# Prompt attention: each round's scores ahead of its transposes on TensorE

## What is computed

```python
s = jnp.einsum('...qkgd,...skd->...kgqs', qg, k)
s = s * (hd ** -0.5) + rel_bias(dist, rel_table)
s = jnp.where(mask, s, -jnp.inf)          # 0 <= dist <= 128, valid keys
m = jnp.maximum(jnp.max(s, axis=-1, keepdims=True), sink)
p = jnp.exp(s - m)
den = jnp.sum(p, axis=-1, keepdims=True) + jnp.exp(sink - m)
o = jnp.einsum('...kgqs,...skd->...qkgd', (p / den).astype(v.dtype), v)
```

## Time and profile before

| | us |
|---|---|
| median of 3 runs (2396.84 to 2398.55) | 2398.39 |
| the profiled execution, its own time | 2398.73 |
| its span, first to last instruction | 2396.6 |
| TensorE busy in it | 2374.7 (99%) |
| VectorE busy | 1004.5 (42%) |
| ScalarE busy | 570.8 (24%) |
| GpSimd busy | 112.1 (5%) |

### The profile page before, as it was taken

The page is one execution under the profiler, slowest core; times in us unless marked ns, Lnnn a source line. Parts: engine busy times, 40 slices in busy tenths (PEclk is TensorE's granted clock), DMA queues, the critical chain, the costliest instruction groups (busy, mean ns, idle before and its releaser), DMA issues.

```text
span 2396.6 us, 35127 instructions
## 1 busy us (share of the span) xinstructions
PE 2374.7 (99%) x15129; PEld 2311.1 (96%) x15129; DVE 1004.5 (42%) x1408; ACT 570.8 (24%) x1016; POOL 112.1 (5%) x131
## 2 busy tenths in 40 slices
PE   8999999999999999999999999999999999999998
PEld 8997899999999999999999998889999999999998
DVE  6449724433433333335623325545343343343333
ACT  6549722111111111103310116422111111110111
POOL 1005400000000000000000004100000000000000
PEclk9999999999999999999999999999999999999999
DMA  8621031111111111111321136431111111111112
GB/s 226 86 48 72 11 100 53 36 53 36 53 35 53 42 46 52 36 45 43 102 65 36 36 108 178 135 124 36 53 53 36 53 35 53 46 41 51 36 36 73
DMA packets 133016, 150.30 MB, mean 63 GB/s; under 512 B 33421, under 2 KB 107177, under 8 KB 132764
## 3 DMA queue, kind: packets, MB, share of 16 engines
q1 hardware_dynamic: 129980, 136.11, 19.2%
q0 software_dynamic: 2720, 12.56, 1.7%
q10 hardware_dynamic: 224, 0.30, 0.0%
HBM read 126.50 MB, written 24.47 MB: 63 GB/s over the span
## 4 chain that ended last, share of the span: by engine, by line
PE 96%; DVE 1%; ACT 1%; issue 0%; DMA 0%; DVEq 0%; SPq 0%
PE ps L316 42%; PE ps L323 21%; PE ps L300 8%; PE ps L304 7%; PE ps L301 7%; PE ps L551 1%; PE ps L1033 1%; PE ps L1009 1%; PE ps L990 1%; ACT prob L1101 1%; PE ps L2080 1%; PE ps L1410 1%; PE ps L1411 1%; PE ps L1412 1%; PE ps L2061 1%; PE ps L2065 1%
## 5 line engine op out<-in xcount | busy, mean ns | idle before, releaser
L1537 DVE TENSOR_TENSOR x<-x,ps 128x1074 f32<-128x1074 f32 (+1 forms) x128 | 161.8, 1264 | 453.5 <-PE ps L323 453.5
L264 ACT ACTIVATE w_hi<-raw 128x1024 fp32r<-128x1024 f32 x180 | 187.4, 1050 | 648.6 <-PE ps L323 485.6
L316 PE MATMUL ps<-act_hi,w_hi 128*128 128x352 f32 (+2 forms) x1536 | 334.4, 326 | 0.0
L316 PE MATMUL ps<-act_hi,w_lo 128*128 128x352 f32 (+2 forms) x1536 | 333.7, 325 | 0.0
L316 PE MATMUL ps<-h_hi,w_lo 128*128 128x352 f32 (+2 forms) x1536 | 333.5, 325 | 0.0
L316 PE MATMUL ps<-h_hi,w_hi 128*128 128x352 f32 (+2 forms) x1536 | 333.4, 325 | 0.0
L323 PE MATMUL ps<-act_lo,w_hi 128*128 128x352 f32 (+2 forms) x1536 | 273.7, 324 | 0.0
L1519 DVE SCALAR_TENSOR_TENSOR relu<-ps,rstd 128x1074 f32<-128x1074 f32 (+1 forms) x64 | 81.1, 1266 | 447.4 <-PE ps L323 447.4
L316 PEld LDWEIGHTS ps<-act_hi,w_lo 128*128 128x128 f32 x1536 | 265.0, 189 | 0.0
L316 PEld LDWEIGHTS ps<-h_hi,w_lo 128*128 128x128 f32 x1536 | 263.8, 189 | 0.0
L316 PEld LDWEIGHTS ps<-h_hi,w_hi 128*128 128x128 f32 x1536 | 263.6, 189 | 0.0
(11 more groups left out here) (324 smaller groups left out, 2363.0 us busy)
## 6 DMA issues: line engine op xcount, KB each, us to landing
raw<-in_mlp_w_up SPq DMA_DIRECT2D x32, 1024.0 KB, 5.5
raw<-in_mlp_w_down SPq DMA_DIRECT2D x32, 1024.0 KB, 5.0
raw<-in_mlstm_w_in SPq DMA_DIRECT2D x12, 1024.0 KB, 5.4
x<-scratch_x SPq DMA_DIRECT2D x8, 537.0 KB, 6.0
scratch_x<-x POOLq DMA_DIRECT2D x1, 4296.0 KB, 14.0
x<-scratch_x SPq DMA_DIRECT2D x8, 528.0 KB, 4.7
x_tok<-in_x_prompt SPq DMA_DIRECT2D x8, 512.0 KB, 7.8
raw<-in_attn_w_qkv SPq DMA_DIRECT2D x16, 256.0 KB, 6.7
```

Of the source, the lines that this page charges most:

```text
L264: nc.scalar.activation(unit_view(w_hi, slot, down), raw_unit(j, rslot, down), ACT.Copy).then_inc(w_hi_ready, 1)
L316: nc.tensor.matmul(ps[:, bank + g, 0:c.stop - c.start], w_block(w, slot, k, kc, cols), hi[:, k, c], start=start and i == 0, stop=False)
L1537: nc.vector.tensor_tensor(view(x[:, o, :]), view(x[:, o, :]), ps[:, out_banks(n):out_banks(n) + 3, 0:w], ALU.add).then_inc(out_free, 1)
```

## The change

In `att_pe`, the transposes of item n-4 are issued behind the scores of item n, except in round 6 where they stay at the head. As the cached keys' transposes and the sample's scores stand ahead of the prompt's scores in the code, the transposes of items 32 to 35 come behind these in rounds 36 to 38.

```diff
         def att_pe(pe):
             for n in range(2, NG + LAG + 1):
-                if LAG + 2 <= n < NG + LAG:
+                if n == LAG + 2:
                     att_transpose_pe(pe, n - LAG)
                 if NG <= n < NG + 2:
                     turn_k_pe(pe, 2 * (n - NG))
...
                 if n < NG:
                     att_scores_pe(pe, n)
+                if LAG + 3 <= n < NG + LAG:
+                    att_transpose_pe(pe, n - LAG)
                 if n == 3:
```

## The result

The median went from 2398.64 us (20 runs) to 2401.7 us (20 runs): a ratio of 1.0014 with an interval of 1.0008 to 1.002. That is 3.1 us or 0.13%, inside the 0.2% that was called no change, and inside the range; the value forecast was 2400.7. The profiled execution took 2402.25 us, its span is 2400.1. Behind the edit the lines are two higher (L1009, L990 and L1033 stay; L1085 is now L1087, L1129 now L1131, L1149 now L1151, L1260 now L1262, L1266 now L1268, L1301 now L1303, L1410 now L1412).

What follows compares the result with a forecast made beforehand. TensorE bounds the kernel, busy 2374.7 of 2396.6 us. First rounds -0.65, middle +1.2 and -0.5 make about 0; the tail adds 2.35: +2.3 us, 2400.7, range 2397.3 to 2403.5.

Steps and rivals of the forecast that it cites:

- The bound and the sign: Attention stage: under 4 us of TensorE stalls to win; whole change forecast slower by 2.3 us.
- A steady round: Full rounds: S, T, V still takes 3.11 us; ScalarE and VectorE run 1.06 us later.
- Rival 3: Every round longer, 3.11 to say 3.25 us, through semaphore latency: 3.9 us atop 2.3, 2404.6; chance 0.05.
- First rounds: Round 7: S(7) fills T(3)'s 1.49 us wait; V(2) starts about 188.5 instead of 189.15, gain 0.65 us.
- Middle: V(14)'s wait behind VectorE's spreading grows, +0.65 to +1.2, taken 1.2; T(20), T(24) give -0.5; sum to round 35 about 0.
- S can fill both: T(20)'s 0.18 and T(24)'s 0.51 us waits for ScalarE are filled by scores: -0.5 to -0.7, taken -0.5.
- no wait: Steady rounds: S never waits for the minimum pass two rounds back, done at t+3.9 against 6.2.
- Tail: Rounds 36 to 39: stalls of 1.65 us ahead of cache transposes and 0.6 ahead of sample's scores; V(35) +2.35 us.
- The lower bound: End of the stage: cost of the new order if ScalarE and VectorE were not late, +1.2 us.
- Rival 1: Tail hidden from the shift, gaps of T(3), T(20), T(24) filled: -0.6 us, 2398.1; chance 0.30 together with no change.
- Rival 2: Rounds 37 and 38: stall plus transposes drop the clock to half, losing 3.4 us atop 2.3: 2404.1; chance 0.08.

Runs made afterwards that it cites:

- experiment 8: The best version: kernel before with T(3), T(20), T(24) behind their scores and only the spreading's clearing moved to round 9; 2395.87 us against 2398.51, ratio 0.9994.
- experiment 1: Kernel before with only T(32) to T(35) behind the sample's work, T(3) to T(31) still ahead of the scores; 2400.13 us, ratio 1.0011.
- experiment 2: Kernel before with only T(3) to T(31) behind the scores, T(32) to T(35) still ahead of the sample's work; 2399.72 us, ratio 1.0009.
- experiment 3: Changed kernel with T(33) alone moved back ahead of the cache transposes of round 37; 2400.7 us, ratio 1.0012 against the kernel before.
- the second of 7: Kernel before with VectorE's spreading moved from round 18 to rounds 9, 10, 11 and T(3), T(20), T(24) behind their scores; ratio 1.0.
- third kernel of experiment 7: Kernel before with VectorE's spreading moved from round 18 to rounds 9, 10, 11 and T(3) to T(31) behind their scores; ratio 1.0008.
- experiment 6: Kernel before with only T(3), T(20) and T(24) behind their scores; 2397.8 us against 2397.49, ratio 0.9997.

## Why the prediction was right, and where it was off

**The bound and the sign** held. The stage had under 4 us to win, and it lost 3.19 (forecast 2.3), less than the 4.8 us that counted as a change. The size is right in part by luck: in the middle a gain of 0.7 us and waits of 0.8 us, neither of which the forecast had, nearly cancel.

**A steady round, 3.11 us and a shift of 1.06 us**: held to the digit. The denominator was put at about t+5.27 or just behind, and stands at t+5.30; the copy and the minimum pass are each 1.06 us later. VectorE's waits for the last exponential rose from 3.0 us in 5 times to 5.8 in 14, the mark of an engine that now follows another. Rival 3 (every round longer) falls with it: from V(14) to V(18) each V stands the same 0.08 us ahead of before.

**First rounds**: -0.65 forecast; what stands ahead of V(2) began 4.93 us from T(2) instead of 5.71, -0.78, and V(2) itself 5.24 instead of 6.08, -0.84. S(7) waited for item 5's minimum pass, as said. What the forecast put at nothing: rounds 7 to 13 also hold transposes for the values and caches (L853, L858), and they cost less behind T than behind S. Round 8, before and then after:
```profile
190.54 1.09 PE L1009 MATMUL ps<-cst,prob 128*128 128x128 f32 x8
...
192.63 0.44 PE L853 MATMUL ps<-cst,vT 128*128 128x128 f32 x2
193.00 1.09 PE L1033 MATMUL ps<-probT,v_tok 128*64 128x128 f32 x16
```
```profile
190.07 1.14 PE L990 MATMUL ps<-kn,q 64*128 64x256 f32 x8
...
192.06 0.38 PE L853 MATMUL ps<-cst,vT 128*128 128x128 f32 x2
192.37 1.09 PE L1033 MATMUL ps<-probT,v_tok 128*64 128x128 f32 x16
```
From the round's start to V it is 2.46 us before and 2.30 after. Rounds 8 to 12 gain 0.12 to 0.15 us each, so V(9) stands 1.56 us earlier than before.

**Middle**: the sum said 0, it was +0.47 (V(31) at 94.60 instead of 94.13 us from T(2)), in these steps. S(15) waited 0.34 us, which the forecast had not: V(10) is 1.14 us early instead of V(9)'s 1.56. At V(14) the lead went from 1.11 us (V(13)) to 0.08, a loss of 1.03; its wait grew by 1.06 (0.73 to 1.79), as the shift says. So this term, 0.65 to 1.2, taken as 1.2, was sized about right, and the stall ate more lead than the forecast knew of. Then the step "S can fill both" gaps, of T(20) and T(24), failed: both scores waited themselves, 0.29 and 0.50 us, for the minimum pass of two items back, and V(23) stood 0.11 us later than before: +0.19 where -0.5 was taken. S(33) waited 0.29, the rest of the 0.47.

I had freed S of that wait ("no wait", done at t+3.9 against 6.2) with the row of a full round and the pass where it stood before the shift. In the new phase the pass ends near t+5.0, so 1.2 us of room are left, and around the meta blocks two rounds together are shorter by more than that. Rounds 22 and 23, after:
```profile
234.63 1.13 PE L990 MATMUL ps<-kn,q 64*128 64x256 f32 x8
235.69 0.26 PE L1009 MATMUL ps<-cst,prob 16*16 16x16 f32 x4
```
T(18) takes 0.19 us from start to start instead of 1.02, and in round 23 V(18) takes 0.33 instead of 1.03. Without its wait S(24) would start some 4.7 us behind S(22) (it started at 239.64, 5.01 behind), and the pass is not done by then. Rounds 31 and 32 are alike ahead of S(33). In rounds 13 and 14, ahead of S(15), the copies of the transposes for the caches delay VectorE as well. Ahead of round 28 it is another thing: VectorE's small sum of item 25 takes 1.29 us instead of 0.16, and ends with GpSimd's scaling, as in experiment 8; it took 1.29 before the change too.
```profile
247.62 1.89 POOL L1121 TENSOR_TENSOR prob<-prob,stat 128x1024 f32<-128x1024 f32 x1
248.25 1.29 DVE L1093 TENSOR_TENSOR stat<-sinks,stat 128x4 f32<-128x4 f32 x1
```

**Tail**: +2.35 forecast, 2.71 us measured: from V(31) to V(35) it was 277.57 to 288.54, 10.97 us, and is 278.40 to 292.08, 13.68 us. The two waits are right in place and size, 1.60 for 1.65 and 0.62 for 0.6; the wait of T(35) for the copy of T(34), 0.18 (0.25 with the overlap lost), and 0.1 inside the sample's scores were missed. The lower bound, +1.2 for a tail without the shift, was too low as well: experiment 1, which is that tail, gives +1.65. Sum of the parts: 0.47 + 2.71 = 3.18.

**The rivals.** Rival 1 fell at both ends: the gaps only changed hands, and the shift reached the tail. Rival 2, the clock: in round 37, 1.60 us of waiting and 1.9 us of transposes stood in a row, and the windows after say 1.00 there:
```profile
275.00:285.00 10.00, 7.78 (x92) 6.65 (x91) 7.81 (x29) 8.12 (x25) 5.68 (x3) 1.00 0.19 57
310.00:311.00 1.00, 1.00 (x8) 1.00 (x8) 0.00 (x0) 0.00 (x0) 0.00 (x0) 0.59 0.00 0
316.00:317.00 1.00, 1.00 (x5) 1.00 (x5) 0.00 (x0) 0.00 (x0) 0.00 (x0) 0.50 1.01 412
317.00:318.00 1.00, 1.00 (x8) 1.00 (x7) 0.00 (x0) 0.00 (x0) 0.00 (x0) 0.99 1.02 417
```
The clock stayed at 2.4 GHz; the first fall is the one of before: it begins at 310.2, during the sample's values, and ends at 317.0. The Trainium skill's "TensorE: Matmul & The Clock Gate" ("Part 4: PE-mode transpose") says that transposes do not count as activity the way matmuls do. No fall followed here, so this stretch of fp32 transposes doesn't bear it out, or it was too short to show it.

**What stays open**: the account of the scores' waits behind the meta blocks (two short rounds) is read from the trace, not tested by an edit, and so is GpSimd's part in the slow small sum and the slow copies. Why a pair of transposes costs less behind T than behind S is not shown.

## What to carry to other kernels

Here three engines ran within 0.2 us of the same period, and swapping two groups on one of them didn't change the period, only the phase of the engines that follow. In such a case read who is a microsecond later, and follow that to every place where the pattern breaks (short items, an inserted job, the end). A group of work that stands ahead of a wait is its cover: when it is moved behind, the wait shows at full length and the group's own followers are late as well. In this kernel only the groups that wait were worth moving: three moved groups of transposes took 0.74 us off the stage, all 33 of them added 3.19. And work that is taken out of an engine's list frees its time only if what stands behind it can start earlier and run as fast: 0.9 us of clearing gave 0.25.

## What the runs showed that I had not expected

The kernel's time comes in steps. The half-rate stretch of TensorE that begins during the sample's values lasted 6.8 us before (306.3 to 313.2) and after, but 3.4 us in the profile of experiment 1:
```profile
308.00:309.00 1.00, 1.00 (x9) 1.00 (x9) 0.00 (x0) 0.00 (x0) 0.00 (x0) 0.77 0.00 0
309.00:311.00 2.00, 2.00 (x9) 2.00 (x9) 0.99 (x4) 1.68 (x5) 0.00 (x0) 0.50 0.39 54
311.00:312.00 1.00, 1.00 (x5) 1.00 (x5) 0.72 (x1) 0.25 (x1) 0.00 (x0) 0.52 0.90 322
```
3.4 us less at half rate are 1.7 us of time, and that profile's span is 2396.4 us although its stage is 1.65 us longer than before (2396.6). Over all twelve profiles the stretch is 3.4 us in five (experiments 1, 2, 3, the second of 7, and 8), 6.8 in six, and 10.2 in the third kernel of experiment 7, whose mean clock is 0.997. The 20 runs of the changed kernel fall into the same steps: 2399.9 to 2400.4 (8 runs, mean clock 0.999), 2401.6 to 2402.3 (8 runs, 0.998), 2402.9 to 2403.6 (4 runs, 0.997), with nothing between. So two single spans can differ by the whole effect of such a change, and the interval of a ratio over mixed steps is as wide as the effect. Compared at the same mean clock, 0.999, with the kernel before in the same comparison, the times follow the stage: the best version's median is 2395.74 against 2396.85, -1.1 us for -1.04 of its stage; experiment 6's is 2396.08 against 2397.06, -1.0 for -0.74; experiment 1's is 2398.63 against 2397.06, +1.6 for +1.65. These are medians of 3 to 16 runs.
